# Cross attention: three heads' probabilities turned by 16-bit DMA transposes, and the first half of its output projection multiplied head by head

## What is computed

```python
def _mem_xattn(h, mem, w_xq, w_xkv, w_xo):
    q = _heads(h @ w_xq, XATTN_HEADS)                      # 4 heads x 256
    k, v = jnp.split(mem @ w_xkv, 2, axis=-1)
    k, v = _heads(k, XATTN_HEADS), _heads(v, XATTN_HEADS)
    s = jnp.einsum('bhsd,bhmd->bhsm', q, k).astype(jnp.float32) * (XATTN_HEAD_DIM ** -0.5)
    p = jax.nn.softmax(s, axis=-1).astype(v.dtype)
    return _merge(jnp.einsum('bhsm,bhmd->bhsd', p, v)) @ w_xo
...
    x = _layer_norm(DEEPNORM_ALPHA * x + xa, ln2_g[l], ln2_b[l])
```

## Time and profile before

| | us |
|---|---|
| median of 3 runs | 393.6 (393.37 to 393.78) |
| profiled execution, device time | 393.74 |
| profiled execution, span of the trace | 391.8 |
| PE busy | 386.1 (99%) |
| DVE busy | 350.1 (89%) |
| ACT busy | 266.9 (68%) |
| POOL busy | 89.6 (23%) |
| granted TensorE clock, mean | 1.00 |

### The profile page before, as it was taken

The page is one execution under the profiler, slowest core; times in us unless marked ns, Lnnn a source line. Parts: engine busy times, 40 slices in busy tenths (PEclk is TensorE's granted clock), DMA queues, the critical chain, the costliest instruction groups (busy, mean ns, idle before and its releaser), DMA issues.

```text
span 391.8 us, 5609 instructions
## 1 busy us (share of the span) xinstructions
PE 386.1 (99%) x2068; PEld 328.8 (84%) x2068; DVE 350.1 (89%) x450; ACT 266.9 (68%) x345; POOL 89.6 (23%) x83
## 2 busy tenths in 40 slices
PE   9999999999999999999999999999999999999995
PEld 5888888888888888889988888888888888888883
DVE  5599599969999885969898898999999999999997
ACT  6567487986354628546773758888887877788841
POOL 2049545254950205001005300000000000000003
PEclk9999999999999999999999999999999999999999
DMA  8997739985635290664747465687777767775202
GB/s 297 372 362 256 254 106 265 264 340 186 233 120 215 66 341 25 221 208 144 207 158 270 135 232 143 216 239 239 234 224 231 228 205 234 239 234 197 50 2 107
DMA packets 31585, 81.27 MB, mean 207 GB/s; under 512 B 8038, under 2 KB 9670, under 8 KB 27462
## 3 DMA queue, kind: packets, MB, share of 16 engines
q1 hardware_dynamic: 28720, 76.39, 57.0%
q0 software_dynamic: 2160, 3.93, 5.8%
q10 hardware_dynamic: 678, 0.59, 0.5%
HBM read 78.28 MB, written 1.05 MB: 202 GB/s over the span
## 4 chain that ended last, share of the span: by engine, by line
PE 96%; DVE 2%; DMA 1%; issue 0%; ACT 0%; DVEq 0%
PE bank L1702 17%; PE bank L1703 17%; PE bank L1704 16%; PE bank L2075 13%; PE bank L1761 13%; PE bank L1765 7%; PE bank L2082 7%; PE bank L1888 2%; PE bank L1708 1%; DMA raw<-in_lead 1%; DVE X L1656 1%; PE bank L1926 0%; DVE stats L1647 0%; PE bank L1954 0%; PE bank L2003 0%; PE bank L1859 0%
## 5 line engine op out<-in xcount | busy, mean ns | idle before, releaser
L1106 DVE TENSOR_TENSOR w_lo<-raw,w_hi 128x2048 fp32r<-128x2048 f32 x30 | 71.4, 2393 | 6.8 <-ACT w_hi L679 6.8
L679 ACT CAST w_hi<-raw 128x2048 fp32r<-128x2048 f32 x32 | 60.5, 1914 | 12.7 <-PE bank L1704 11.1
L2075 PE MATMUL bank<-actA,w_hi 128*128 128x512 f32 x224 | 55.4, 390 | 0.0
L2075 PEld LDWEIGHTS bank<-actA,w_hi 128*128 128x128 f32 x224 | 42.0, 188 | 8.7
L642 POOL DMA_DIRECT2D raw<-in_w_ff x15 | 13.2, 879 | 155.7 <-DMA raw<-in_w_ff 155.7
L1702 PE MATMUL bank<-w_hi,actB 128*128 128x512 f32 x107 | 42.6, 398 | 0.0
L1703 PE MATMUL bank<-w_lo,actB 128*128 128x512 f32 x107 | 41.8, 391 | 0.0
L1704 PE MATMUL bank<-w_hi,actB 128*128 128x512 f32 x107 | 41.8, 390 | 0.0
L1761 PE MATMUL bank<-actA,w_hi 128*128 128x512 f32 x156 | 38.3, 392 | 0.0
L1702 PE MATMUL bank<-w_hi,actA 128*128 128x512 f32 x96 | 37.9, 395 | 0.0
L1704 PE MATMUL bank<-w_hi,actA 128*128 128x512 f32 x96 | 37.4, 390 | 0.0
(11 more groups left out here) (254 smaller groups left out, 887.8 us busy)
## 6 DMA issues: line engine op xcount, KB each, us to landing
raw<-in_w_ff SPq DMA_DIRECT2D x32, 1024.0 KB, 5.2
raw<-in_w_in SPq DMA_DIRECT2D x10, 1024.0 KB, 6.8
raw<-in_w_xkv SPq DMA_DIRECT2D x8, 1024.0 KB, 5.9
raw<-in_w_mix_o SPq DMA_DIRECT2D x4, 1024.0 KB, 4.9
raw<-in_w_xq SPq DMA_DIRECT2D x4, 1024.0 KB, 5.1
raw<-in_w_xo SPq DMA_DIRECT2D x4, 1024.0 KB, 5.6
raw<-in_w_ff POOLq DMA_DIRECT2D x15, 256.0 KB, 5.1
raw<-in_lead SPq DMA_DIRECT2D x6, 384.0 KB, 4.9
```

Source lines behind the costliest of these rows:

```text
L679: act.copy(dst, half_view(u)).then_inc(hi_done, 1)
L1106: dve.tensor_tensor(dst, half_view(u), hi_part.bitcast(f32), ALU.subtract).then_inc(lo_done, 1)
L2075: pe.matmul(b[:, :].rearrange("p (h s) -> p h s", h=2), hi[:, k, m * P:(m + 1) * P], actA[:, :, k, :], start=k == 0, stop=False, skip_grou ...
```

## The change

The probabilities of heads 0, 1 and 2 are no longer turned on PE. For each of them POOL copies the head's 512 numbers a partition into two planes of 512 words (8 blocks of 128x128 words; into `values`, where the head's query stood, so it waits for the head's scores as well), SP issues a DMA transpose back into `qk`, ACT joins the words in `values` (`join_cross`), and ACT and DVE split the result as before, now reading it from `values` instead of a bank. Head 3 is still turned on PE. The first half of the output projection is no longer multiplied bank by bank: the blocks `k` 0 and 1 (head 0) of three banks come first, then head 1's values, the fourth bank, the turn of head 3, then `k` 2 and 3 (head 1) of two banks, head 2's values, the third, head 3's values, the fourth. ACT's and DVE's programs are reordered to match.

```diff
+TURNED_HEADS = 3
...
+            def turn_cross(h):
+
+                sp.wait_ge(cross_planes_made, h + 1)
+                wait_full(sp, f"cs{h}")
+                sp.dma_start(cross_words[h].rearrange("p (g q) -> p g q", q=P), cross_planes[h], transpose=True)\
+                    .then_inc(cross_turned_in[h], 16)
+
+            turn_cross(0)
             wait_lo(sp, FIRST_DOWN_UNIT - RAW)
             sp.dma_start(half_view(FIRST_DOWN_UNIT), w_ff2[0]).then_inc(raw_in[FIRST_DOWN_UNIT % RAW], 16)
+            turn_cross(1)
             load(unit(C_FF1_0, 0), w_ff1[0], 4)
+            turn_cross(2)
             sp.wait_ge(ln_done, 4)
             load_ln(1)
...
+            def make_cross_planes(h):
+
+                pool.wait_ge(cprob_done, 2 * h + 2)
+                wait_full(pool, f"cs{h}")
+                pool.tensor_copy(cross_planes[h].rearrange("p (x n) -> p x n", x=2),
+                                 cross_words[h].rearrange("p (n x) -> p x n", x=2)).then_inc(cross_planes_made, 1)
+
+            make_cross_planes(0)
+            make_cross_planes(1)
             add_b22(0)
+            make_cross_planes(2)
...
+            def join_cross(h):
+
+                act.wait_ge(cross_turned_in[h], 16)
+                act.copy(cross_planes[h].rearrange("p (n x) -> p x n", x=2),
+                         cross_words[h].rearrange("p (x n) -> p x n", x=2)).then_inc(cross_joined, 1)
...
+                if h < TURNED_HEADS:
+                    act.wait_ge(cross_joined, h + 1)
+                    act.copy(cprobsT_hi[:, h].rearrange("p m (t q) -> p m t q", t=2),
+                             cross_joint[h].rearrange("p (t m q) -> p m t q", t=2, m=2)).then_inc(cT_hi_done, 1)
+                    return
...
             cexps(1)
+            join_cross(0)
             cT(0)
...
             cq(3)
+            cross(0)
+            cexps(2)
+            seed_cross(1)
+            join_cross(1)
             cT(1)
-            cexps(2)
-            cross(0)
+            cexps(3)
             cross(1)
+            hi_half(15, 0)
+            join_cross(2)
             cT(2)
-            cexps(3)
-            seed_cross(1)
-            hi_half(15, 0)
-            cross(2)
             cT(3)
             hi_half(15, 1)
+            cross(2)
             cross(3)
...
             cscore(1)
-            ctranspose(0)
             two_blocks(13, 2, ["xq30", "xq31"])
             cscore(2)
-            ctranspose(1)
...
             cvalues(0)
             cscore(3)
...
+            cross_rows(0, 0, 0)
+            cross_rows(0, 1, 0)
+            cross_rows(1, 0, 0)
             cvalues(1)
-            ctranspose(2)
...
+            cross_rows(1, 1, 0)
+            ctranspose(3)
+            wait_lo(pe, unit(14, 1))
+            wait_out(pe, "cpv1")
+            cross_rows(0, 0, 2)
+            cross_rows(0, 1, 2)
+            cvalues(2)
+            cross_rows(1, 0, 2)
+            cvalues(3)
+            cross_rows(1, 1, 2).then_inc(rows_used, 1)
             wait_out(pe, "cpv2")
             wait_out(pe, "cpv3")
             rows(15, 1, B, xo, 4, 4, between={(3, 2): lambda: transpose_x(1, 0, "yt", [0]), (3, 3): lambda: transpose_x(1, 0, "yt", [1])})
```

More of the change, by code:

```diff
@@ L338, in by_word @@
             return v.rearrange("p (h n x) -> p h x n", h=2, x=2)
+        cross_words = [qk[:, 512 * h:512 * (h + 1)].bitcast(u16) for h in range(TURNED_HEADS)]
+        cross_joint = [values[:, 512 * h:512 * (h + 1)] for h in range(TURNED_HEADS)]
+        cross_planes = [v.bitcast(u16) for v in cross_joint]
         def by_plane(v):
@@ L370, in build @@
         turned_in = [sem(f"turned_in{j}") for j in range(HA // 2)]
+        cross_planes_made, cross_joined = sem("cross_planes_made"), sem("cross_joined")
+        cross_turned_in = [sem(f"cross_turned_in{h}") for h in range(TURNED_HEADS)]
         mix_hi = sem("mix_hi")
@@ L383, in build @@
         cq_hi_done, cT_hi_done = sem("cq_hi_done"), sem("cT_hi_done")
+        cT_lo_done = sem("cT_lo_done")
         cross_hi = sem("cross_hi")
@@ L962, in down_high @@
                     wait_full(act, "cs3")
+                    act.wait_ge(cT_lo_done, TURNED_HEADS)
                 elif q == 1:
@@ L1413, in cT @@
             def cT(h):
+                dve.wait_ge(cT_hi_done, h + 1)
+                if h < TURNED_HEADS:
+                    dve.wait_ge(cross_joined, h + 1)
+                    dve.tensor_tensor(cprobsT_lo[:, h].rearrange("p m (t q) -> p m t q", t=2),
+                                      cross_joint[h].rearrange("p (t m q) -> p m t q", t=2, m=2),
+                                      cprobsT_hi[:, h].bitcast(f32).rearrange("p m (t q) -> p m t q", t=2),
+                                      ALU.subtract).then_inc(cT_lo_done, 1)
+                    return
                 b = wait_full(dve, f"cpt{h}")
-                dve.wait_ge(cT_hi_done, h + 1)
                 dve.tensor_tensor(cprobsT_lo[:, h], b[:, :].rearrange("p (m s) -> p m s", m=2),
@@ L1485, in _ @@
             cmaxes(2)
+            cross(0)
+            cnorm(2)
+            cmaxes(3)
             cT(1)
-            cnorm(2)
-            cross(0)
-            cmaxes(3)
+            t2_sum(0)
+            cnorm(3)
             cross(1)
+            t1_t4_sums(0)
+            lo_half(15, 0)
             cT(2)
-            cnorm(3)
-            t2_sum(0)
-            t1_t4_sums(0)
+            cT(3)
+            lo_half(15, 1)
             cross(2)
-            cT(3)
-            lo_half(15, 0)
-            lo_half(15, 1)
             cross(3)
@@ L2007, in cvalues @@
                 b = begin(f"cpv{h}")
-                wait_out(pe, f"cpt{h}")
+                if h < TURNED_HEADS:
+                    pe.wait_ge(cT_lo_done, h + 1)
+                else:
+                    wait_out(pe, f"cpt{h}")
                 for d in range(2):
@@ L2035, in _, with cross_rows @@
             cscore(3)
-            cvalues(1)
-            ctranspose(2)
[L2038 to L2046, removed]
+            xo = ["xo00", "xo01", "xo10", "xo11"]
+            def cross_rows(t, n, first):
+                b = bank[FILL[xo[2 * t + n]][0]]
+                if first == 0:
+                    pe.wait_ge(seeded, 4 + 2 * t + n + 1)
+                for k in range(first, first + 2):
+                    i = three(b[:, :], [a[:, k, t * P:(t + 1) * P] for a in B],
+                              weight_rows(14, k, n * 512, (n + 1) * 512), False, False, on=True)
+                return i
+            wait_lo(pe, unit(14, 0))
+            wait_out(pe, "cpv0")
+            cross_rows(0, 0, 0)
+            cross_rows(0, 1, 0)
+            cross_rows(1, 0, 0)
+            cvalues(1)
+            cross_rows(1, 1, 0)
[8 more added lines that the diff above has]
+            cross_rows(1, 1, 2).then_inc(rows_used, 1)
             wait_out(pe, "cpv2")
```

## The result

| | kernel before | changed kernel |
|---|---|---|
| median | 393.49 us (4 runs, 393.31 to 393.78) | 398.42 us (4 runs, 398.07 to 398.65) |
| ratio to before, 95% interval | | 1.0121 [1.0109, 1.0133] |
| profiled execution / its span | 393.74 / 391.8 | 398.65 / 396.6 |

The change costs 4.9 us where +2.0 was forecast. The direction was right; the time lies just above the range, whose upper end was 398.1.

The account below looks back on a forecast made before the run. PE bounds the kernel, busy 99% of the span and without gaps in 170 to 216 us. -1.32 + 0.6 + 0.05 + 1.1 + 0.2 + 1.4 = +2.0 us: 395.8 profiled, 395.6 as median; range 394.0 to 398.1.

Parts of the forecast that it names:

- The turns removed: Three heads no longer turned on PE, 0.44 us a head: -1.32 us.
- (1): PE before head 3's scores: the query's low part comes later while PE arrives sooner, a wait of 0.6 us.
- The turn-taking between POOL and DVE: Each new POOL copy holds a DVE instruction with both operands in SBUF by 0.9 us.
- (2): PE before head 1's values: wait of 0.05 us if the transpose issued at 186.7 has landed by 190.9.
- the term for the DMA transpose's landing: DMA transpose of 8 blocks: 3.4 to 3.7 us from issue to landing.
- the rival of late landings: Head 1's transpose takes 6.4 us, the wait before its values grows to 2.3, time 397.9 us; chance 0.17.
- (3): PE before head 2's values: waits 1.1 us for ACT's cast, DVE's low part of chunk 15's first block, then the split.
- (4): PE before the projection's second half: waits 0.2 us for ACT's and DVE's read-out of head 3's values.
- (5): Turn of the normed tokens (X) inside the second half: X ready at S + 10.9, PE at S + 9.5, wait 1.4 us.
- the prediction's estimate of 10.5 us: Eight 128x128 DMA turns in a row at 1309 ns each: 10.5 us, sum +12; chance 0.02.

Follow-up runs that it names:

- three moves: Changed kernel with add_b22(0) behind POOL's third copy, down block's cast before heads 2 and 3's read-outs, head 2's join and split before chunk 15's first block: 398.19 us.

## Why the prediction was wrong in size

What bounds the kernel was read rightly: PE has no slack, and every microsecond of new wait showed in the time. The turns removed gave what was priced: PE is ready for the scores of head 3, behind two turns fewer, at 187.80 us. The whole stretch starts 0.25 us later than before, so that compares as 187.55 with 188.41: 0.86 us for two turns. The mean spacing of the 128x512 matmuls in the stretch is 0.229 us against 0.228, under 0.1 us in all.

**(1) Scores of head 3**, 0.6 forecast, 0.86 measured. The turn-taking between POOL and DVE read from the earlier trace rows is there: POOL's copies took

```profile
L668 POOL COPY values<-qk x3: 1032/1432/1436, 176.3 to 191.4; 128x1024 uint16<-128x1024 uint16 x3
```

and the two DVE subtractions beside the first one, in the kernel before and in the changed one,

```profile
175.88 1.28 DVE L1398 TENSOR_TENSOR again<-probsT,again 128x512 fp32r<-128x512 f32 x2
...
176.14 2.12 DVE L1442 TENSOR_TENSOR again<-probsT,again 128x512 fp32r<-128x512 f32 x2
```

took 2.12 us, 1.28 in the kernel before: 0.84 us for one copy, where 0.9 was estimated. Only the first copy cost that. The second, at 185.56, began inside a subtraction with both operands in SBUF and took 1.44 us, but no DVE instruction beside it was longer than in the kernel before. The third took 1.03 us and held only a small DVE instruction (L1478, 0.50 us instead of 0.17). The two copies that met such a subtraction took 1.43 and 1.44 us, so by the rule of shared interfaces that the prediction took from the GPSIMD Engine Reference of the Trainium skill (the table at the start), the trace agrees. Of the 0.26 us above the forecast, 0.15 lies between the end of the query's low part on DVE, at 188.52, and PE's start at 188.67, which the sum left out.

**(2) Values of head 1**, 0.05 forecast, 1.58 measured: this is the step that failed, by the term for the DMA transpose's landing, 3.4 to 3.7 us forecast and 6.0 measured. Its condition, "if the transpose, issued at 186.7, has landed by 190.9", was not met; it was issued at 187.02 and landed 6.0 us later. I had taken 3.4 to 3.7 us "since for heads 0 and 1 no weight load is queued ahead", which held for head 0 (3.0 us), and had set `add_b22(0)` at 0 by asking only when that load itself would land. What it does to the transpose issued beside it was not in the sum, only in the rival of late landings, at 0.17. That rival is what happened: it named the accumulating load, gave 6.4 us for the landing and 397.9 for the time. The lateness also leaves 0.3 us behind the turn of head 3, a place that the sum didn't have. The experiment with the load moved gave back 2.3 us.

**(3) Values of head 2**, 1.1 forecast, 1.09 measured; **(4) start of the second half**, 0.2 and 0.29; **(5) turn of X**, 1.4 and 1.22. For (3) and (5) the trace names the releaser that was forecast, and each went with the one move that its reason calls for. For (4) it names none, and no run takes that wait away. Behind the start of the second half the turn began after 10.86 us, where X was forecast for 10.9, and PE was free for it after 9.64 us, where 9.5 was forecast: that is most of what (5) is short of. DVE's idle time ahead of the down block was forecast at 1.2 us, and is 1.04.

**Joins and blocks.** The join took 1.36 us, as scaled from the earlier trace rows. The page VectorE: DVE Perf Modes of the Trainium skill (The three transpose paths) gives 1309 ns for one 128x128 turn by DMA; eight of them in a row, the prediction's estimate of 10.5 us, are not what the trace shows. 8 blocks landed 3.0 us after the issue, 0.38 us each with all fixed cost in it, so that figure is not a price per block in a row of them.

**The sum.** Of the 2.9 us between forecast (395.8) and result (398.65) of the profiled execution, (2) is 1.5 and its after-effect 0.3; (1), (4) and (5) make +0.26, +0.09 and -0.18; restarts about 0.3, the start of the run 0.27. That makes 2.6; the rest is open. The range missed by 0.3 us: the late landing stood as an end of it, without the larger wait of (1), the restarts and the start on top.

## What to carry to other kernels

A DMA that an engine waits for is priced with everything that is in flight when it is issued, on every queue: ask not only when the neighbour lands, but what it does to this one. Taking work off the bounding engine helps only as far as the engines behind it have time to spare; here 1.3 us came off PE, while the query of head 3 and the normed tokens had been ready 0.8 us before they were wanted, and the added steps used up more than that. Moves that each help alone have to be laid out together again before they are combined, since each was tried in one order only: three moves that brought 2.3, 1.5 and 1.4 us alone brought 0.2 us together, and the first two of them 3.1.

## What the runs showed of the hardware

- A DMA transpose of 8 blocks of 128x128 16-bit words within SBUF lands 3.0 us after its issue, 4.8 us with an accumulating load from POOL issued 0.1 us ahead, 6.0 us with a 1 MB load 1.3 us behind it too. That load behind it alone costs nothing; a 1 MB load 4 us ahead gave 4.5 us, one 0.55 us ahead 5.9 us.
- POOL's copy of 1024 words takes 1.03 us, and 1.43 when it begins inside a DVE subtraction with two SBUF operands. Of the three copies one held the next such subtraction by 0.84 us, one held a small DVE instruction by 0.33 us, and one held none.
- A PE wait of 3.0 us was followed by matmuls of 128x512 at 0.43 us from start to start in one kernel (granted clock 0.53 over 2.9 us) and at 0.23 in another; one of 5.8 us by the lower level over 6 us. Behind waits of 1.6 us and less the granted clock stayed at 1.00.
- Behind a wait the first matmul takes 0.08 us more until the next one starts, at a granted clock of 1.00; behind a turn on PE it does so without a wait (191.65 to 191.96 in the kernel before, where 0.23 is usual).
